# A DRAM table of expert rows laid out by rounds of 32 rows, so that each block of 128 rows is one run

## What is computed

```python
def moe_ffn(h, w_router, router_bias, w_gate, w_up, w_down):
    scores = sigmoid(h @ w_router)                      # (384, 16)
    ... # best of 4 groups of 4 experts, then the 2 best experts of that group
    gates = sum(one_hot(idx, 16) * w[..., None], axis=-2)
    a = einsum('bld,edf->blef', h, w_gate)              # 16 experts, 1024 -> 256
    u = einsum('bld,edf->blef', h, w_up)
    return einsum('blef,efd->bld', silu(a) * u * gates[..., None], w_down)
```

## Time and profile before

| what | value |
|---|---|
| time, median of 3 runs | 1336.86 us (1333.83 to 1338.5) |
| profiled execution, its own time | 1333.37 us |
| its span in the trace | 1331.4 us |
| PE busy | 951.5 us, 71% |
| VectorE, ScalarE, GpSimd busy | 374.3, 297.1, 49.6 us |
| chain that ended last | PE 50%, DMA 27%, DVE 12%, ACT 5% |
| ScalarE's DMA queue (blocks of rows) | 25.36 MB, 4.9% of 16 engines |
| SyncE's DMA queue (weights) | 185.68 MB, 36.9% of 16 engines |

### The profile page before, as it was taken

One profiled execution on the slowest core, in us unless ns is written; L12 is line 12 of the kernel. 1 busy time (PEld: TensorE's weight loads), 2 busy tenths in 40 slices (PEclk: granted clock), 3 DMA queues, 4 the chain that ended last, 5 costly groups with the idle time before them and its releaser, 6 DMA issues.

```text
span 1331.4 us, 13746 instructions
## 1 busy us (share of the span) xinstructions
PE 951.5 (71%) x5481; PEld 488.7 (37%) x5481; DVE 374.3 (28%) x908; ACT 297.1 (22%) x690; POOL 49.6 (4%) x62
## 2 busy tenths in 40 slices
PE   5999887877668984385828715998998438591971
PEld 2456555653444542121203203554454212130321
DVE  0331065763455013010101005346622301010112
ACT  2320232243346013010101004116731201010111
POOL 0300000000000001000000000000001100000001
PEclk8899988887889996597868956996999659796895
DMA  9999965255540222457667842040003245675724
GB/s 396 423 419 412 414 264 194 93 188 210 183 146 1 94 96 95 167 223 234 256 222 283 353 169 85 0 169 29 1 7 136 102 164 222 237 279 198 291 103 158
DMA packets 35089, 256.86 MB, mean 193 GB/s; under 512 B 2800, under 2 KB 2944, under 8 KB 20048
## 3 DMA queue, kind: packets, MB, share of 16 engines
q1 hardware_dynamic: 16848, 185.68, 36.9%
q0 software_dynamic: 11696, 44.91, 8.6%
q10 hardware_dynamic: 6480, 25.36, 4.9%
HBM read 203.17 MB, written 52.77 MB: 192 GB/s over the span
## 4 chain that ended last, share of the span: by engine, by line
PE 50%; DMA 27%; DVE 12%; ACT 5%; issue 3%; POOL 1%; ACTq 0%; POOLq 0%; SPq 0%; DVEq 0%
DMA expert_rows<-U 21%; PE ps L456 17%; PE ps L568 8%; PE ps L805 5%; DMA U<-expert_rows 4%; PE ps L590 3%; PE ps L470 2%; PE ps L420 2%; PE ps L552 2%; DMA ring<-w_in 1%; PE ps L495 1%; PE ps L724 1%; DVE U L1529 1%; PE ps L477 1%; PE ps L516 1%
## 5 line engine op out<-in xcount | busy, mean ns | idle before, releaser
L568 PE MATMUL ps<-ring,U 128*32 128x512 f32 x1200 | 176.8, 614 | 56.1 <-DVE U L1395 56.1
L568 PE MATMUL ps<-hT,U 128*32 128x512 f32 x168 | 81.3, 642 | 37.0 <-DVE U L1395 37.0
L456 PE MATMUL ps<-U,ring 128*128 128x384 f32 x320 | 105.1, 487 | 2.7 <-DVE U L1309 1.4
L568 PEld LDWEIGHTS ps<-ring,U 128*32 128x32 f32 x1200 | 47.2, 114 | 149.3 <-issue 91.3
L590 PE MATMUL ps<-ring,U 128*32 128x512 f32 x672 | 93.5, 634 | 10.1 <-ACT U L970 10.1
L1395 DVE COPY U<-ps 128x512 f32<-128x512 f32 x24 | 16.6, 691 | 266.8 <-DMA expert_rows<-U 216.7
L552 PE MATMUL ps<-small,U 128*128 128x128 f32 x192 | 32.0, 318 | 74.7 <-DMA U<-expert_rows 72.6
L568 PE MATMUL ps<-U 128*32 128x512 f32 x168 | 81.3, 642 | 0.0
L456 PEld LDWEIGHTS ps<-U,ring 128*128 128x128 f32 x320 | 60.1, 189 | 47.4 <-issue 4.2
L970 ACT COPY U<-ps 128x512 f32<-128x512 f32 x24 | 14.1, 585 | 256.4 <-DMA expert_rows<-U 221.9
L805 PE MATMUL ps<-ring,hT 128*128 128x384 f32 x192 | 65.9, 503 | 5.7 <-ACT hT L883 4.9
(11 more groups left out here) (246 smaller groups left out, 1311.2 us busy)
## 6 DMA issues: line engine op xcount, KB each, us to landing
ring<-w_in SPq DMA_DIRECT2D x102, 1536.0 KB, 11.1
expert_rows<-U POOLq DMA_DIRECT2D x15, 2048.0 KB, 75.0
U<-expert_rows ACTq DMA_DIRECT2D x24, 512.0 KB
expert_rows<-U ACTq DMA_DIRECT2D x24, 512.0 KB
hT<-w_in SPq DMA_DIRECT2D x6, 1536.0 KB, 8.5
U<-w_in SPq DMA_DIRECT2D x6, 1536.0 KB, 13.2
small<-small_in SPq DMA_DIRECT2D x1, 3147.5 KB, 34.5
xT<-x_in SPq DMA_DIRECT2D x1, 1536.0 KB, 16.7
```

What stands on the lines that cost most here:

```text
L456: ins = mm(out, lhs(k), rhs(k), start=(k == 0), stop=(k == n - 1))
L568: ins = mm(ps[q:q + 32, r, :], xgT[:, r, P * k + q:P * k + q + 32], w[e][:, c:c + 512], start=(k == 0), stop=(k == DC - 1))
```

## The change

`CAP` goes from 480 to 512. The table is laid out by rounds: first the rows 0 to 31 of all sixteen experts, then the rows 32 to 63 of all, and so on. The four experts of a group lie beside each other, so a block is 128 consecutive rows of DRAM, and `block_of` is a plain slice. The row number is no longer the key itself: VectorE casts the key (expert * 512 + place) to an integer and puts its bits together anew, `(key >> 9) << 5 | (key & 480) << 4 | (key & 31)`.

```diff
-CAP = 480
+CAP = 512
...
+        key_i, key_e, key_r = (rt[:, 792 + 6 * i:798 + 6 * i].bitcast(mybir.dt.int32) for i in range(3))
...
-        block_of = lambda rows, i: rows.rearrange("(e s) n -> e s n", e=NE)[GS * (i // NR):GS * (i // NR) + GS, 32 * (i % NR):32 * (i % NR) + 32, :]
-        by_expert = lambda tile: tile
-        beyond_rows = lambda rows, e, b: rows[bass.ds(e * CAP + (NR * 32 + P * b), P), :]
+        block_of = lambda rows, i: rows[32 * NE * (i % NR) + P * (i // NR):32 * NE * (i % NR) + P * (i // NR) + P, :]
+        beyond_rows = lambda rows, e, b: rows.rearrange("(r q) n -> r q n", q=32 * NE)[NR + 4 * b:NR + 4 * b + 4, bass.ds(e * 32, 32), :]
...
-                    act.dma_start(by_expert(xgb[i % NR]), block_of(rows_d, i)).then_inc(xg_full[i % NR], 16)
+                    act.dma_start(xgb[i % NR], block_of(rows_d, i)).then_inc(xg_full[i % NR], 16)
...
-                    act.dma_start(block_of(rows_d, i), by_expert(ysb[i % 2])).then_inc(y_stored[i % 2], 16)
+                    act.dma_start(block_of(rows_d, i), ysb[i % 2]).then_inc(y_stored[i % 2], 16)
...
-                dve.tensor_copy(row_of, row_f).then_inc(S["rows_ready"], 1)
+                link(dve.tensor_copy(key_i, row_f))
+                ts(key_e, key_i, 9, 5, ALU.logical_shift_right, ALU.logical_shift_left)
+                ts(key_r, key_i, 480, 4, ALU.bitwise_and, ALU.logical_shift_left)
+                link(ts(key_i, key_i, 31, None, ALU.bitwise_and))
+                link(tt(key_e, key_e, key_r, ALU.bitwise_or))
+                tt(row_of, key_e, key_i, ALU.bitwise_or).then_inc(S["rows_ready"], 1)
```

## The result

The changed kernel takes 1163.87 us (median of 4 runs, 1157.83 to 1170.82) beside 1335.34 us for the kernel before (median of 4 runs; three of them gave the 1336.86 us above). The ratio is 0.8718, with a 95% interval of 0.8664 to 0.8772. The profiled execution took 1170.82 us, the longest of the four, with a span of 1168.9 us: 162.5 us less than the profiled one before.

The account below looks back on a forecast made before the run. Block transfers using four of sixteen DMA engines, which also carry weights, bound the expert stage. Savings of 163.8 us less 1.8 added made 162.0, taking the profiled 1333.4 to 1171.4, median about 1175; range 1150 to 1200, 70 in 100.

Parts of the forecast that it names:

- row numbers on VectorE: Before the scatter: five added VectorE instructions cost 0.9 us a layer, 1.8 us in all, fully on the path.
- Start: Scatter to first `up`: third block lands at 546.7, `up` starts at 548.8; 12.1 us less in layer 0, 12.4 in layer 1.
- Body: Groups of the expert stage: 148 us a layer, for 217.8 and 202.4 before; 69.8 and 54.4 us less.
- weights against it: Within the body: 42.5 MB at 377 GB/s make PE wait 8 us for weights, with 0 and 16 as ends.
- Stores within a group: Expert stage: block stores cost nothing, since two `down`s (7 us) and the next `up` cover them.
- the rival of the held queue: Expert stage: ScalarE's queue stays held in each group, 64 us in all, 1239 us; 5 in 100.
- Last store: End of each expert stage: 5.4 us for 14.78 in layer 0, 4.2 for 9.86 in layer 1.
- Clearing: Beside the input projection: the sixteenth clearing transfer costs nothing; 5.1 us if the weights' lead in the ring were used up.
- Weights as the harder bound: Expert stages: at 300 GB/s weights make PE wait 37 us a layer, 1233 us; from about 1200 up, 17 in 100.
- Scatter and gather: Rival: power-of-two strides in DRAM lengthen scatter and gather by 2.75 us each, 11 us in two layers, 1186 us; 3 in 100.
- Block transfers of 2 to 6 us: Sign in the expert stage: each block's load or store takes 2 to 6 us if the change works as forecast.
- no chain step of over 10 us on `expert_rows`: Sign in the profile's chain: no step on transfers with the row table exceeds 10 us.

Follow-up runs that it names:

- experiments 1 and 2: Kernel before, old table, each block moved by four transfers of 32 rows (1): 1205.12 us; by two transfers of 2 by 32 rows (2): 1540.74 us.
- Experiment 5: Changed kernel, with SyncE's queue holding the two freed weight slots until PE has turned the first three blocks: 1149.09 us, ratio 0.8623.
- experiment 6: Changed kernel, zeros from oTy and slots held: 1144.81 us; also layer 1's first weights held until layer 0's stores: 1157.20 us, or until its gather: 1129.71 us.

## Why the prediction was right, point by point

| term | foreseen, us | profile, us |
|---|---|---|
| start of the stages, layers 0 and 1 | -12.1, -12.4 | -12.1, -13.5 |
| body, layers 0 and 1 | -69.8, -54.4 | -75.2, -62.8 |
| last store, layers 0 and 1 | -9.4, -5.7 | -5.3, -7.1 |
| row numbers on VectorE, both layers | +1.8 | +1.5 |
| clearing, and the rest up to the first scatter | 0 | +12.1 |
| sum | -162.0 | -162.4 |

A body runs here from the first `up` to the copy of the last half result.

The mechanism was right: four engines of sixteen were the bound, and experiments 1 and 2 move the time both ways by the number of engines alone. The sum agrees better than its terms deserve, because two errors cancel: the body came out 13.8 us shorter than foreseen, and the stretch before the first scatter 12.1 us longer. It also compares one profiled execution with one. I added 3.5 us to get from the profiled execution to the median, 1175 us; here the profiled one was the longest of four, and the median is 1163.87, 171.5 us less than before. That the foreseen 1171.4 us met the profiled 1170.8 so closely is luck. (The text names 1200 and 1210 as upper end; the result lies inside either.)

- *Start.* From the scatter's landing to `up` 16.84 us, foreseen 16.85. The split is not quite mine: I had the third block land 14.8 us after the scatter and one block turned behind it; PE's last wait ended 12.9 us after it, and two blocks were turned behind (3.87 us). Experiment 5 shows that the two slots made up 7.9 of the 16.8 us.
- *Body.* The step "weights against it" was mis-sized. I took a wait of 8 us a layer from the rate of the mixed stretch (377 GB/s); PE waited 0.8 us in both layers, since the stretch runs at 420. That the low rate of before belonged to a load that lay unevenly on the engines is my reading; no run separates it. PE's own work is as summed: 139.7 us in layer 1 for 139.9.
- *Stores within a group.* "Cost nothing" holds for groups 0 to 2 and fails at the end of layer 0. Stores take 9.9 us at the median, more than the 2 to 6 I named, and no wait of PE follows within the groups. But the last copy of layer 0 waits for the store of two blocks ago, and starts at 704.37, 3.1 us after the last `down` is done; no next `up` is there to cover it. ScalarE's issues fell to 0.34 us, so the rival of the held queue is out.
- *Last store.* In layer 0 it takes 9.49 us for 5.4: it shares the engines with weights, which experiment 6 shows. In layer 1, alone, 2.78 for 4.2.
- *Clearing.* "I cost it at nothing" is the step that failed. I named GpSimd's first sum as the first to need the clears and missed VectorE's wait on `row_cleared`, which stands in the code (line 1510 before) and which the trace of before doesn't show, because there the last clear landed at 176.6 us and VectorE came at 181.7. The upper price I gave, 5.1 us, was the time of all engines for 2.1 MB; but the clears share the engines with the weights. Sixteen of them took from 44.3 to 187.2 us, 235 GB/s, at which one more costs 9 us (an estimate from these rows), and the last landed 10.6 us later than before. The wait was 8.9 and 13.5 us, and PE went on at a lower granted clock behind it (0.50 from 186 to 200 us, with 47 matmuls for 93 before at 1.00). The 12.1 us in order: the changed kernel was 3.5 us ahead when VectorE reached the wait, 5.4 us behind after it, 9.1 us behind at 230 us and 12.1 us at the scatter. The last 3 us aren't explained.
- *Weights as the harder bound* came only half: PE waits for them 0.3 to 0.4 us a layer. *Scatter and gather* took 11 us as before, so the power-of-two stride doesn't show. (That rival's sum was wrong: at three quarters of the rate 11.0 us grow by 3.7 and not by 2.75, in all 14.7 and 1190 us.)
- *Signs that did not come.* "Block transfers of 2 to 6 us" and "no chain step of over 10 us on `expert_rows`": loads took 11.4 us at the median, and 12.5 and 11.7 us stand in the chain at the start of the stages. The second sign contradicted the sum, which had the third block land 13 us behind the issue. The groups came every 35.5 us, just under the 36 named.

## What to carry to other kernels

Look at the mean busy share of the DMA engines while a single transfer is waited for: 0.25 is four engines of sixteen, and 0.13 is two. Cut transfers so that the slowest dimension is the 128 partitions; four transfers of 32 use all engines and still lose 40 us here. When a buffer is made larger, search the code for every wait on its semaphore, since a wait that is met in time, here with 5 us to spare, stands in no row. And once the engines are full, what matters is what is issued beside a short transfer that someone waits for: holding back bulk weights gave some 28 us more (14 at the start of the stages, 14 at the end of layer 0), holding them to the wrong moment cost 12.

## What the runs showed of the hardware beyond that

- With blocks moved as four transfers of 32 partitions beside the weights, all sixteen engines were busy (1.01) and moved 326 to 348 GB/s in the stretches with stores, for 420 with one transfer of 128, wherever the rows lay in DRAM.
- A block transfer of 512 KB took 2.7 us alone and 9.5 us beside streaming weights. The last rows of a gather issued together with eight slots of weights landed after 28.8 us for 6.
- Two transfers that each use two engines take the same two: a share of 0.12 to 0.13 while they ran, and 210 us longer than one transfer that uses four.
- A sixteenth clear of 2.1 MB beside streaming weights moved the last landing by 10.6 us, for 5.1 us of all engines' time.
